# Decode attention over a paged key cache: keys turned in 32x32 blocks on VectorE, four steps scored in one burst

## The reference, cut to what matters

```python
k_full = cache_k[page_table].reshape(Bd, n_cand, MOBA_BLOCK, N_KV_HEADS, HEAD_DIM)
kmean  = mean(k_full, axis=2)
gate   = einsum('btcgd,bncd->btcgn', q, kmean)         # one gate a block
_, sel = top_k(gate, 3)
s_sel  = einsum('btcgd,btcgsd->btcgs', q, k_sel) * scale
s_own  = einsum('btcgd,bscd->btcgs', q, k_new) * scale  # the new tokens, causal
p      = softmax(concat([s_sel, s_own]))
o      = einsum(p[..., :nsel], v_sel) + einsum(p[..., nsel:], v_new)
```

## Time and profile before

| | us |
|---|---|
| median of 3 runs | 3027.46 (3019.6 to 3027.55) |
| the profiled execution | 3028.81 |
| its span, first to last instruction | 3027.1 |
| TensorE busy in the span | 2936.3 (97%) |
| VectorE busy | 2001.3 (66%) |
| ScalarE busy | 836.6 (28%) |
| stage of the change, 970 to 1253 us: TensorE busy | 273.70 of 283 |

### The profile page before, as it was taken

One profiled execution on the slowest core, in us unless ns is written; L12 is line 12 of the kernel. 1 busy time (PEld: TensorE's weight loads), 2 busy tenths in 40 slices (PEclk: granted clock), 3 DMA queues, 4 the chain that ended last, 5 costly groups with the idle time before them and its releaser, 6 DMA issues.

```text
span 3027.1 us, 53548 instructions
## 1 busy us (share of the span) xinstructions
PE 2936.3 (97%) x20734; PEld 2385.0 (79%) x20734; DVE 2001.3 (66%) x3792; ACT 836.6 (28%) x1961; POOL 298.6 (10%) x520
## 2 busy tenths in 40 slices
PE   8999999999999999997999999999999999999997
PEld 7888788887775677786888888888888877878776
DVE  4444466658997433168666766667676689787887
ACT  1000144431328534113222222222222233222234
POOL 0000011100002555151000000000000000000002
PEclk8999999999999999998999999999999999999999
DMA  6333100013212999701323233232332335342221
GB/s 178 83 84 84 32 10 11 11 45 84 84 49 79 284 284 282 241 18 61 130 74 129 97 105 129 72 130 89 115 116 85 101 120 189 100 141 89 89 89 74
DMA packets 338064, 322.60 MB, mean 107 GB/s; under 512 B 20601, under 2 KB 323686, under 8 KB 336408
## 3 DMA queue, kind: packets, MB, share of 16 engines
q1 hardware_dynamic: 323284, 278.66, 29.7%
q0 software_dynamic: 14528, 40.52, 4.3%
HBM read 296.37 MB, written 22.74 MB: 105 GB/s over the span
## 4 chain that ended last, share of the span: by engine, by line
PE 83%; DVE 12%; ACT 2%; issue 2%; DMA 0%; POOL 0%; SPq 0%; DVEq 0%; POOLq 0%; ACTq 0%
PE ps L1392 46%; PE ps L852 11%; PE ps L921 7%; PE ps L1221 4%; PE ps L1362 4%; PE ps L777 2%; PE ps L1174 2%; PE ps L1303 1%; PE ps L1260 1%; PE ps L1286 1%; ACT BIG L1833 1%; DVE W L2477 0%; DVE BIG L2476 0%; DVE BIG L2478 0%; DVE W L2475 0%
## 5 line engine op out<-in xcount | busy, mean ns | idle before, releaser
L1392 PE MATMUL ps<-BIG,UA 128*128 128x272 f32 x2288 | 538.9, 392 | 0.4 <-ACT UV L2021 0.4
L1392 PEld LDWEIGHTS ps<-BIG,UA 128*128 128x128 f32 x2288 | 434.6, 190 | 90.4 <-issue 0.8
L1392 PE MATMUL ps<-XT,UA 128*128 128x272 f32 x1400 | 331.6, 392 | 0.0
L1392 PEld LDWEIGHTS ps<-XT,UA 128*128 128x128 f32 x1400 | 266.0, 190 | 54.8
L1392 PE MATMUL ps<-BIG,DA 128*128 128x272 f32 x1200 | 293.7, 393 | 9.6 <-ACT UV L2122 3.2
L1392 PEld LDWEIGHTS ps<-BIG,DA 128*128 128x128 f32 x1200 | 226.5, 190 | 59.9 <-issue 12.1
L777 PE MATMUL ps<-XT,W 128*128 128x272 f32 x768 | 180.4, 395 | 0.7 <-ACT W L1783 0.7
L777 PEld LDWEIGHTS ps<-XT,W 128*128 128x128 f32 x768 | 146.7, 192 | 35.1 <-issue 4.8
L921 PE MATMUL ps<-BIG 64*64 64x64 f32 (+1 forms) x3072 | 141.4, 230 | 12.7 <-issue 4.9
L921 PEld LDWEIGHTS ps<-BIG 64*64 64x64 f32 x3072 | 122.9, 134 | 24.8 <-issue 12.4
L3564 POOL COPY CVT<-GP 128x2 f32<-128x2 f32 x44 | 15.5, 352 | 1005.3 <-DVE GP L3015 822.3
(11 more groups left out here) (655 smaller groups left out, 5374.4 us busy)
## 6 DMA issues: line engine op xcount, KB each, us to landing
BIG<-in_w_up_dram SPq DMA_DIRECT2D x176, 512.0 KB, 5.8
W<-in_w_in_dram SPq DMA_DIRECT2D x38, 1024.0 KB, 5.8
BIG<-in_w_down_dram SPq DMA_DIRECT2D x96, 384.0 KB, 3.8
W<-in_cache_k_dram SPq DMA_DIRECT2D x128, 128.0 KB, 3.5
W<-in_cache_k_dram POOLq DMA_DIRECT2D x128, 128.0 KB, 3.6
W<-in_cache_v_dram SPq DMA_DIRECT2D x128, 128.0 KB, 3.4
W<-in_cache_v_dram POOLq DMA_DIRECT2D x128, 128.0 KB, 3.5
h_keep<-H SPq DMA_DIRECT2D x22, 544.0 KB, 2.7
```

What stands on the lines that cost most here:

```text
L1392: last = nc.tensor.matmul(ps[:, bank, 0:HALF], weights[:, k], x[:, k], start=start and k == 0, stop=k == kc - 1, skip_group_check=not start)
```

## The change

The transposes on TensorE go. A key page lies one token to a partition, and VectorE turns each 32x32 block of four pages in place, one instruction over 128x1024 for each request and step (`turn_keys` on VectorE, 64 in all). Partition 32g + d then holds, for the 32 tokens of row group g, dimension d (of 32) of a kv head's half. The scores are then taken with 32x32 tiles: 4 row groups (tokens) times 4 column groups (request, pair of kv heads), each row group into its own PSUM bank, accumulated over four terms (2 kv heads by 2 halves of 64 dimensions), 64 matmuls for a burst of four steps. To that end the queries are spread by matmuls with parts of the identity (`spread_queries`) and copied into a zeroed, masked layout (`sample_queries`); the new keys likewise (`own_keys`).

Key pages get a buffer of four steps for each request (all of W), which is free when the burst is scored; value pages get two steps for each request. Scores leave PSUM in four copies a burst without sums; VectorE sums and takes maxima for all four steps together (`block_stats`). The own scores of all pairs are done in slots 1 and 4. `LAG` goes from 2 to 3, so value step v is weighed in slot v + 11 and multiplied in slot v + 12; `HALF_SLOT` and the order of the page list change.

```diff
-        LAG = 2
+        LAG = 3
         V_FROM = 8 + LAG
         CACHE_SLOTS = 32 + V_FROM + 1
-        HALF_SLOT = [7, 11, 13, 15, 17, 19, 21, 23, 25, 27, 29, 31, 33, 35, 38]
+        HALF_SLOT = [4, 6, 8, 10, 12, 14, 16, 18, 20, 22, 24, 26, 28, 30, 34]
+        BURST = 4
+        PAGE_STEPS = []
+        for _g in range(0, CACHE_SLOTS, BURST):
+            _k = [("k", t, t) for t in range(_g, _g + BURST) if t < 32]
+            _v = [("v", t - V_FROM, t) for t in range(_g, _g + BURST) if 0 <= t - V_FROM < 32]
+            PAGE_STEPS += _k[0:1] + _v[0:1] + _k[1:2] + _v[1:2] + _k[2:] + _v[2:]
+        HALF_LOAD = {PAGE_STEPS.index(("k", 4, 4)): (0, 1), PAGE_STEPS.index(("k", 6, 6)): (2,), PAGE_STEPS.index(("k", 8, 8)): (3,)}
         for _i in range(4, 16):
-            _s = SLOT_STEP[HALF_SLOT[_i - 4] + 1] + 4
+            _t = HALF_SLOT[_i - 4] + 2
+            _s = PAGE_STEPS.index(("v", _t - V_FROM, _t) if _t >= V_FROM else ("k", _t, _t))
             HALF_LOAD[_s] = HALF_LOAD.get(_s, ()) + (_i,)
...
         def load_pages(eng, b, fill=None):
...
-                eng.wait_ge(page_free[j], s // 4 + 1)
+                if kind == "k":
+                    x, source, landed = KEYS[b][:, 1024 * (n % BURST):1024 * (n % BURST) + 1024], ck, page_landed[2 * (n % BURST) + b]
+                    if n >= BURST:
+                        eng.wait_ge(S["qk_mm"], n // BURST)
+                    elif b and n == 2:
+                        eng.wait_ge(w3_clear, 1)
+                else:
+                    x, source, landed = VALS[n % 2][b].rearrange("p j n -> p (j n)"), cv, v_landed[2 * (n % 2) + b]
+                    if n >= 2:
+                        eng.wait_ge(v_free[b], n)
+                    else:
+                        eng.wait_ge(S["ao_mm"], 8)
...
         # TensorE
+            def spread_queries(half, bank):
+                for k in range(4):
+                    for g in range(4):
+                        last = nc.tensor.matmul(ps[32 * g:32 * g + 32, bank, k * P:(k + 1) * P], ident[:, 32 * k:32 * k + 32],
+                                                ZT[:, 0:8, SEQ + 16 * half:SEQ + 16 * half + 16], start=True, stop=True, skip_group_check=True)
+                return last
...
+            def scores(n):
+                pe.wait_ge(S["kt_ev"], 2 * BURST * (n + 1))
+                pe.wait_ge(S["sc_ev"], 4 * n + 4)
+                if BURST * n + BURST > HALF_SLOT[0]:
+                    pe.wait_ge(acc_free, IN_TILES + 2 + sum(s < BURST * (n + 1) for s in HALF_SLOT))
+                for k in range(4):
+                    for b in BOTH:
+                        for r in BOTH:
+                            o, h = 32 * (2 * b + r), 2 * r + k // 2
+                            keys = KEYS[b].rearrange("p (j h c t) -> p h c j t", h=4, c=2, t=32)[:, h, k % 2]
+                            for g in range(4):
+                                rows = slice(32 * g, 32 * g + 32)
+                                last = nc.tensor.matmul(ps[o:o + 32, g, :], QB[n // 4][rows, n // 2 % 2 * 2 + b, h, k % 2], keys[rows],
+                                                        start=k == 0, stop=k == 3, skip_group_check=True)
                 last.then_inc(S["qk_mm"], 1)
...
             for t in range(CACHE_SLOTS):
                 v = t - V_FROM
-                if 0 < t < 32:
-                    turn_keys(t)
-                if t < 32 and t % 8:
-                    scores(t - 1)
...
                 if 0 < v <= 32:
                     values(v - 1)
...
                 if t in HALF_SLOT:
                     half_tile(HALF_SLOT.index(t))
+                if t < 32 and t % BURST == BURST - 1:
+                    scores(t // BURST)
...
         # VectorE
+            def turn_keys(t):
+                for b in range(2):
+                    dve.wait_ge(page_landed[2 * (t % BURST) + b], 64 * (t // BURST) + 64)
+                    x = KEYS[b][:, 1024 * (t % BURST):1024 * (t % BURST) + 1024]
+                    nc.vector.transpose(x, x).then_inc(S["kt_ev"], 1)
+            for t in range(BURST):
+                turn_keys(t)
             dve.wait_ge(S["ao_ev"], 8)
...
             for t in range(CACHE_SLOTS):
                 v = t - V_FROM
+                if t % BURST == 0 and 0 < t <= 32:
+                    for i in range(t - BURST, t):
+                        block_stats(i)
+                if t % 8 == 0 and 0 < t <= 32:
+                    dve.wait_ge(S["own_ev"], (t - 8) // 16 + 2)
+                    softmax_terms(t // 8 - 1)
+                if t % BURST == BURST - 1 and BURST <= t < 32:
+                    turn_keys(t)
                 if t - 1 in HALF_SLOT:
                     half_tile(HALF_SLOT.index(t - 1))
+                if t % BURST != BURST - 1 and BURST <= t < 32:
+                    turn_keys(t)
```

More of the change, by code:

```diff
@@ L465, in load_pages @@
             eng.wait_ge(S["page_in"], 16)
-            for u in range(SLOTS):
+            for u in range(2 * b, 2 * b + 2):
                 eng.wait_ge(w_free[u], ROUND_OUT[u] + 1)
-            for s, kind, n in PAGE_STEPS:
+            eng.wait_ge(v_free[b], 1)
+            for s, (kind, n, _) in enumerate(PAGE_STEPS):
                 bp, i = divmod(n, 8)
@@ L580, in _ @@
                     sp.wait_ge(w_free[u], ROUND_OUT[u] + 1)
-                    for b in range(2):
-                        sp.wait_ge(page_free[2 * u + b], 17)
+                    sp.wait_ge(S["qk_mm"], 32 // BURST)
                 else:
@@ L1129, in _ @@
             keys_values(4, 6)
-            for j in range(6):
-                pe.sem_inc(page_free[j], 1)
+            for b in range(2):
+                pe.sem_inc(v_free[b], 1)
             def pair_scores(q, group):
@@ L1264, in own_scores @@
-            def own_scores(bp):
-                pe.wait_ge(S["dec_ev"], max(bp, 1))
-                if bp:
-                    pe.wait_ge(S["ptd_ev"], 9 * bp - 8)
-                pe.wait_ge(S["gn_root"], 2 * PAIRS + 1)
-                for b in BOTH:
-                    for r in BOTH:
-                        o = 32 * (2 * b + r)
-                        last = nc.tensor.matmul(ps[o:o + 32, 6, 0:N_DEC], qb(r, 2 * bp + b), ZT[:, 8 + r, SEQ:TOK], start=True, stop=True, skip_group_check=True)
+            pe.wait_ge(S["max_ev"], 64)
@@ new lines, in _, with own_keys, own_scores @@
+            pe.wait_ge(S["qk_laid"], 2)
+            def own_keys():
+                for k in range(4):
+                    last = nc.tensor.matmul(ps[0:32, 6, 64 * k:64 * k + 64], ident[:, 32 * k:32 * k + 32], ZT[:, 8:10, SEQ:TOK],
+                                            start=True, stop=True, skip_group_check=True)
+                last.then_inc(S["own_mm"], 1)
+            def own_scores(half):
+                if half == 0:
+                    pe.wait_ge(S["own_ev"], 1)
+                else:
+                    pe.wait_ge(S["qk_laid"], 3)
+                for i in BOTH:
+                    for b in BOTH:
+                        for r in BOTH:
+                            o = 32 * (2 * b + r)
+                            for k in range(4):
+                                last = nc.tensor.matmul(ps[o:o + 32, 6, N_DEC * i:N_DEC * (i + 1)], QB[half][0:32, 2 * i + b, 2 * r + k // 2, k % 2],
+                                                        KOWN[:, k, r], start=k == 0, stop=k == 3, skip_group_check=True)
+                last.then_inc(S["own_mm"], 1)
@@ L1937, in _ @@
                         block_exp(t // 8 - 1, n)
[L1938 to L1941 removed]
+                if t < 32 and t % BURST == BURST - 1:
+                    score_copy(t // BURST)
             turned(3)
```

269 lines of the change are left out of this document (115 added, 154 removed).

## The result

The changed kernel takes 3089.0 us (median of 4 runs, 3085.8 to 3094.3) against 3026.3 for the kernel before: a ratio of 1.0213, 95% interval 1.0192 to 1.0235. It is slower by 63 us, about the time by which TensorE was relieved on paper; forecast were 3061 us and a range to 3092 (the forecast's own range ended at 3085). The profiled execution took 3087.65 us, its span 3086.0 against 3027.1.

What follows compares the result with a forecast made beforehand. TensorE was taken to set the pace, DMA engines 8% behind. Five standstill terms summed to 82.0 us against 48.4 now: 33.6 later, 3028.8 to 3062.4, less 1.3 over the median, 3061 us; range 3006 to 3092, own range 3040 to 3085.

Steps and rivals of the forecast that it cites:

- rival D: VectorE's in-place transposition holds the queue: 3077 us at 2.45 each, 3139 if POOL could not issue meanwhile; chance 0.10.
- the sum of 82.0: Forecast total standstill of POOL's page queue in the changed kernel, in us, added over five stretches of the stage.
- the 48.4: Standstill of POOL's page queue in the kernel before: 277.9 us for its 256 pages against 229.5 undisturbed.
- (a): First burst, keys only: pages out at 972.3, queue waits until the burst ends near 995; standstill 22.7 us.
- (b): Second burst, only keys loading: last keys land at about 1014.5, burst ends at 1021.6; standstill 12.2 us.
- (c): Third burst: landing 2.7, transposes 1.9, evacuation 0.7, burst with handoff 4.1; standstill 9.4 us.
- (d): Five full bursts of keys and values: 6.0 us standstill each, cycles of 34.8 us; 29.9 in all.
- the 1.7 us for the DMA engines: Per full cycle, extra time to bring 8.39 MB: 26.9 us at 313 GB/s against 25.2 of issuing.
- (e): Last eleven value steps with two buffers: 2.2 us, plus 5.6 for slot 34's half tile; standstill 7.8 us.
- C: In TensorE's bursts, tiles overlap only by four: each burst 11.3 us longer, +90, 3150 us; chance 0.07.
- A: Pages run ahead and TensorE's relief of 63 us counts: 3010 us, or 3000 with an earlier first burst; chance 0.18.
- B: No change, 3028 us: the shorter full cycles repay the standstill at the start; chance 0.10.

Runs made afterwards that it cites:

- the last version: Against the kernel before: the change with bursts of two, first early, half tiles respread, four tail value buffers, lag 2, earlier turns, delayed output weights, dummy products; 3033.3 us, 1.0027.

## Why the prediction was right, and where it was too small

The mechanism and the sign were right. The time lies in the range, 28 us above the forecast and 3 below the range's end; it is above the 3085 at which the forecast's own range ended. The range reached 3092 to take in half of rival D, which did not come true, so that the time lies inside is in part luck. By the prediction's own steps:

- **The number to count.** Standstill of the page queue explains 58 of the 59 us. TensorE's relief was no gain, as forecast. But the sum of 82.0 adds up waits for engines, and the 48.4 that it is held against holds other things too. The 48.4 are 38.4 of waits, 6.0 in three gaps of 0.9 to 2.6 us that the profile puts down to no engine, and 4.0 of pages a little over 0.90 us apart. The changed kernel has nearly the same: 5.5 in such gaps (0.9, 2.2 and 2.4) and 4.5 of spacing. The sum put these 10 us at nothing without a reason. One of the gaps, in the kernel before:

```profile
1085.25 0.55 POOL L476 DMA_DIRECT2D W<-in_cache_v_dram  x1 [2.94 <-issue]
```

- **(a)** Forecast end of the first wait 995, measured 994.34. That fits in part by luck: the pages began 3.5 us sooner and the eight transpositions ended 4.0 sooner (979.4), but from there to the burst's end it took 14.0 us instead of 11.6, at a granted clock of 0.55 from 980 to 990. The wait itself is 25.4 instead of 22.7.
- **(b)** 16.8 instead of 12.2. The burst took 6.6 us at a lowered clock, not 3.9; four transpositions (4.63 us) stood behind the landing of k6, not two behind that of k7; and the first page went out 0.95 us after the burst's end, which the sum had at nothing. The landing on which VectorE waited came sooner than the counted one, 3.8 us after the queue was free instead of 5.1.
- **(c)** 12.4 instead of 9.4. A page of k10 on SyncE's queue took 7.1 us to land, so that VectorE, which turns in order, had four transpositions left (4.74 us) instead of one to two (1.9). Counted from when POOL was free the landing is 1.5, less than the 2.7 of the sum; the burst with the 0.95 to the next page is 5.4 instead of 4.1.
- **(d)** Four waits, not five: no key page follows the last burst. They are 6.5, 5.4, 6.8 and 8.1, together 26.8 where 29.9 were counted for five and 24 for four. So this term fits by luck. The landings are not what was short: 4.4 to 5.4 us from issue where 3.6 were counted, but the 1.7 us for the DMA engines had paid for that (though not as a bound: 347 GB/s were moved between 1100 and 1110 us, above the 313 of the prediction). A burst and the 0.95 to the next page took 5.4 instead of 4.1.
- **(e)** 15.1 instead of 7.8. The half tile's part is as counted (5.8 against 5.6). The rest is 9.3 instead of 2.2: value products ahead of most of these waits ran at the lower clock, 1.8 to 2.0 us instead of 1.08, and again 0.95 to the next page. The landings there, 3.0 to 4.2 us from issue, are as counted.
- Waits together 96.5 instead of 82.0. Behind the last page 3.1 more, the last half tile at 10.1 us.

So of the 24.5 us by which the standstill came out larger than the sum, 10.0 are what the sum left out, and 14.5 are links of the chain. Two things come back among these: the 0.95 us from the end of TensorE's work to the next page, where 0 to 0.2 were counted, in (b) to (e); and the lower clock in (a), (b), the first full cycle of (d), and (e). The 3 to 10 us allowed for the clock were in the range and not in the sum; the estimate above says 14 to 17. The run with idle work warns against the reverse: it brought the clock back in one stretch, and no time.

Of the rivals, C is out: a burst took 4.46 us, nearer to 16 tiles side by side (3.9) than to four (15.2). The Trainium skill (TensorE: Matmul & The Clock Gate, Part 3: Packing small matmuls) has a factor of 10.6 for 16 tiles, from which the prediction estimated 5.5; the trace lies between the two. D is out as well (its 3077 was counted from 3062.4, not from 3061). The transposition took 1.23 us where 1.22 was counted, and POOL's pages went out at their spacing while VectorE turned (timeline of the changed kernel):

```profile
1176.31 2.36 DVE L2594 STREAM_TRANSPOSE W<-W 128x1024 f32<-128x1024 f32 x2
1176.80 0.55 POOL L488 DMA_DIRECT2D W<-in_cache_k_dram  x1 [0.35 <-issue]
1177.72 0.55 POOL L488 DMA_DIRECT2D BIG<-in_cache_v_dram  x1 [0.37 <-issue]
```

The lock that the Trainium skill describes (SBUF — State Buffer, SBUF: two separate sides) is thus not seen with this operation. A and B failed on (a) to (c): only with a smaller burst did the full cycles run ahead as A wanted, and even then the start cost too much. Of the signs named beforehand, half tiles are 36.0 to 37.5 us apart by four slots in the changed kernel, where 33 to 36 were said, and the stage ended at 1310.8, not near 1286.

What stays open: whether the 8 us that the last version lacks lie wholly in the keys-only stretch. Its standstill is 52.7 us against 48.4, and what follows the last page was not taken apart. Open too is what the lower clock costs by itself outside the stretch in which the dummies brought it back.

## What to carry to other kernels

When work leaves the busiest engine, ask first what the transfers wait for: a buffer that comes free as a whole, behind several links (landing, turning, evacuation, a burst in an engine's program order), stops its queue for the sum of these links less what is issued meanwhile. Cover counts only if nothing ahead of the burst, on any engine or queue, needs those pages too. Price such a chain at the lower clock, with the time from the end of each link to the next issue (here 0.95 us), and hold the sum only against a number that is made of the same parts. Free buffers in small parts: bursts of two, with the page order that follows them, brought back two thirds of the loss, and a second buffer alone 29 us in the runs with half pages.

## What the runs showed of the hardware

- A burst of 64 float32 matmuls on 32x32 tiles took 4.46 us with 512 columns and 2.75 with 256, from which, as an estimate, 1.0 us do not depend on the columns and each of eight rounds of 512 takes 0.43.
- VectorE's 32x32 transposition of 128x1024 in place took 1.23 us, as long as the copy of as many elements out of PSUM that it replaced.
- Between 970 and 980 us TensorE worked 5.3 of 10 us; from 980 to 985 its granted clock was 0.50, the lower of the two levels of 2.4 and 1.2 GHz. Where the clock had fallen, half tiles took 8.4 to 10.3 us instead of 7.57 and value products up to 1.94 instead of 1.08; the second burst took 6.6 instead of 4.46.
- Where POOL's next page waited for TensorE, its DMA began 0.95 to 0.97 us after the end of that work (1025.00 to 1025.95, 1055.77 to 1056.73, 1203.27 to 1204.22); pages that wait for nothing are 0.90 apart.
- POOL's queue has gaps of 0.9 and 2.2 to 2.6 us before its 84th and 114th page in the kernel before and in every version measured, put down to no engine; the cause is open.
